# Buffers of the dense matmuls at multiples of 1024 bytes, and another order of the small matmuls in a chunked RWKV-7 solve

## The reference

```
h = rms_norm(x, norm_mix[l])
p = h @ w_in[l]                                   # 2048 -> q, k, v, RWKV inputs, two gates
y_attn = sliding_window_attention(q, k_att, v_att, attn_sinks[l])
y_rwkv = rwkv7_time_mix(r, k, v, dw, da, dg, ...)
merged = (sigmoid(gate_a) * (y_attn @ w_branch_attn[l])
          + sigmoid(gate_b) * (y_rwkv @ w_branch_rwkv[l]))
x = x + merged @ w_out[l]
h = rms_norm(x, norm_ffn[l])
x = x + (silu(h @ ffn_gate[l]) * (h @ ffn_up[l])) @ ffn_down[l]
return rms_norm(x, norm_final)
...
def step(S, inp):                                 # inside rwkv7_time_mix, one token, 16 heads
    sa = einsum('bhij,bhj->bhi', S, -kk_t)
    S = (S * w_t[:, :, None, :] + sa[..., None] * (kk_t * a_t)[:, :, None, :]
         + v_t[..., None] * k_t[:, :, None, :])
    return S, einsum('bhij,bhj->bhi', S, r_t)
```

## Time and profile before

| | us |
|---|---|
| median of 3 runs | 3176.09 |
| their range | 3173.41 to 3176.93 |
| the profiled execution, whole | 3174.01 |
| its span, first to last instruction | 3172.2 |
| TensorE busy in it | 3064.1 (97%) |
| GpSimd / VectorE / ScalarE busy | 1108.0 / 1221.9 / 958.5 |
| TensorE's mean granted clock | 0.987 of 2.4 GHz |

### The profile page before, as it was taken

The page is one execution under the profiler, slowest core; times in us unless marked ns, Lnnn a source line. Parts: engine busy times, 40 slices in busy tenths (PEclk is TensorE's granted clock), DMA queues, the critical chain, the costliest instruction groups (busy, mean ns, idle before and its releaser), DMA issues.

```text
span 3172.2 us, 39005 instructions
## 1 busy us (share of the span) xinstructions
PE 3064.1 (97%) x15226; PEld 2434.3 (77%) x15226; DVE 1221.9 (39%) x1380; ACT 958.5 (30%) x1226; POOL 1108.0 (35%) x275
## 2 busy tenths in 40 slices
PE   7999999999899999999999999999999999999997
PEld 5666777777677777788788888888888888888885
DVE  5446362552535436365554331023211222023345
ACT  4344233332333323322223332133212332122221
POOL 4222122231222212344444444444344443444442
PEclk9999999999999999999999999999999999999998
DMA  4112122121221212334334322222223222222222
GB/s 165 67 67 78 50 77 74 57 83 50 77 72 58 83 48 79 117 139 150 121 139 152 119 94 85 100 105 93 93 91 107 93 93 89 95 106 93 93 86 98
DMA packets 63239, 296.30 MB, mean 93 GB/s; under 512 B 6688, under 2 KB 7968, under 8 KB 38688
## 3 DMA queue, kind: packets, MB, share of 16 engines
q1 hardware_dynamic: 55168, 280.17, 25.1%
q10 hardware_dynamic: 7968, 14.68, 1.2%
HBM read 274.12 MB, written 20.71 MB: 93 GB/s over the span
## 4 chain that ended last, share of the span: by engine, by line
PE 83%; issue 6%; DVE 6%; POOL 2%; ACT 2%; DVEq 1%; DMA 0%; POOLq 0%; SPq 0%; ACTq 0%
PE dense L1173 25%; PE dense L1175 23%; PE dense L1174 23%; PE work L1368 2%; POOL wlo L474 2%; PE work L1349 2%; DVEq L788 1%; DVE zq L970 1%; DVE tmp L838 1%; PE work L1358 1%; DVE tmp L973 1%; PE work L1325 1%; PE work L1228 1%; PE work L1263 1%; PE work L1337 0%
## 5 line engine op out<-in xcount | busy, mean ns | idle before, releaser
L474 POOL TENSOR_TENSOR wlo<-raw,whi 128x2048 fp32r<-128x2048 f32 (+1 forms) x254 | 1083.1, 4264 | 2022.7 <-ACT whi L520 2022.7
L1173 PE MATMUL dense<-H_hi,whi 128*128 128x512 f32 x2672 | 1087.4, 407 | 41.2 <-issue 15.2
L1175 PE MATMUL dense<-H_hi,wlo 128*128 128x512 f32 x2672 | 1049.6, 393 | 0.0
L1174 PE MATMUL dense<-H_lo,whi 128*128 128x512 f32 x2672 | 1048.8, 393 | 0.0
L520 ACT ACTIVATE whi<-raw 128x2048 fp32r<-128x2048 f32 (+1 forms) x255 | 454.2, 1781 | 1482.6 <-PE dense L1175 1404.0
L1173 PEld LDWEIGHTS dense<-H_hi,whi 128*128 128x128 f32 x2672 | 506.0, 189 | 189.0 <-issue 63.4
L1175 PEld LDWEIGHTS dense<-H_hi,wlo 128*128 128x128 f32 x2672 | 506.0, 189 | 109.6
L1174 PEld LDWEIGHTS dense<-H_lo,whi 128*128 128x128 f32 x2672 | 507.3, 190 | 100.9 <-issue 5.0
L1173 PE MATMUL dense<-G_hi,whi 128*128 128x512 f32 x704 | 277.4, 394 | 0.0
L1174 PE MATMUL dense<-G_lo,whi 128*128 128x512 f32 x704 | 277.4, 394 | 0.0
L1175 PE MATMUL dense<-G_hi,wlo 128*128 128x512 f32 x704 | 277.4, 394 | 0.0
(11 more groups left out here) (235 smaller groups left out, 2664.4 us busy)
## 6 DMA issues: line engine op xcount, KB each, us to landing
raw<-w_slots SPq DMA_DIRECT2D x103, 1024.0 KB, 4.9
raw<-w_gu SPq DMA_DIRECT2D x88, 1024.0 KB, 4.7
raw<-w_down SPq DMA_DIRECT2D x64, 704.0 KB, 4.0
gates_dram<-gout ACTq DMA_DIRECT2D x32, 256.0 KB, 2.6
gin<-gates_dram SPq DMA_DIRECT2D x16, 512.0 KB, 3.8
X<-xT SPq DMA_DIRECT2D x8, 512.0 KB, 10.7
xin<-xT SPq DMA_DIRECT2D x16, 256.0 KB, 3.4
x_dram<-x ACTq DMA_DIRECT2D x16, 256.0 KB, 3.6
```

What stands on the lines that cost most here:

```text
L474: nc.gpsimd.tensor_tensor(wlo[s][:, 0:cols], raw[s][:, 0:cols], whi[s][:, 0:cols].bitcast(f32), SUB).then_inc(lo_ready, 1)
L1173: PE.matmul(bank[:], whi[s][:, wk], hi[:, k, :], start=(k == first), stop=False)
L1174: PE.matmul(bank[:], whi[s][:, wk], lo[:, k, :], start=False, stop=False)
L1175: done = PE.matmul(bank[:], wlo[s][:, wk], hi[:, k, :], start=False, stop=(k == last))
```

## The change

It does two things.

1. `cst` and `norm_g` come from an arena of their own (`small`) that begins where `keep` began. `keep` begins behind it, at the next multiple of 1024, 19456 = 19 x 1024. So `raw`, `whi`, `wlo`, `H_hi`, `H_lo` and, since all their sizes are multiples of 1024, `M_hi`, `M_lo`, `G_hi`, `G_lo` and `resid` all begin at multiples of 1024. `cst` keeps its remainder of 128. The other buffers of the pairs move from a remainder of 704 to 896.
2. In the solve, W1 comes first for both heads, the head changing with every product, and the sixteen transposes follow in one block. P2 changes head with every product too. The wait before W1 is now for both heads' masked copies. `w1_done` and `x_done` are raised once per level as before, and `p2_done` twice, both at the end of P2. No instruction of arithmetic is added or taken away.

```diff
+OPERAND_ALIGN = 1024
...
-    keep = Arena(nc, -(-nc.sbuf_base // 64) * 64)
+    small = Arena(nc, -(-nc.sbuf_base // 64) * 64)
+    cst = small("cst", [5, P])
+    ident, ones, head_ones, head_mean, head_center = (cst[:, i, :] for i in range(5))
+    norm_g = small("norm_g", [3, KD])
+    keep = Arena(nc, -(-small.at // OPERAND_ALIGN) * OPERAND_ALIGN)
     raw = [keep(f"raw{s}", [SLOT]) for s in range(2)]
     whi = [keep(f"whi{s}", [SLOT], f32r) for s in range(2)]
     wlo = [keep(f"wlo{s}", [SLOT], f32r) for s in range(2)]
     H_hi = keep("H_hi", [KD, T_SEQ], f32r)
     H_lo = keep("H_lo", [KD, T_SEQ], f32r)
-    cst = keep("cst", [5, P])
-    ident, ones, head_ones, head_mean, head_center = (cst[:, i, :] for i in range(5))
-    norm_g = keep("norm_g", [3, KD])
...
                     for level in range(LEVELS):
-                        for e in range(2):
-                            if level:
-                                pe.wait_ge(p2_read, p * (2 * LEVELS) + 2 * level - 1 + e)
-                            for t in range(NB):
+                        if level:
+                            pe.wait_ge(p2_read, p * (2 * LEVELS) + 2 * level)
+                        for t in range(NB):
+                            for e in range(2):
                                 done = PE.matmul(RW[heads[e], t * HALF:(t + 1) * HALF], Ln[:, e, t, :],
                                                  second_halves(Y[:, e, t, :], level),
                                                  start=True, stop=True)
-                            if e:
-                                done.then_inc(w1_done, 1)
+                        done.then_inc(w1_done, 1)
+                        for e in range(2):
                             for t in range(NB):
                                 at = (e * NB + t) * CHUNK
                                 for c in range(2):
...
-                        for e in range(2):
-                            for t in range(NB):
+                        for t in range(NB):
+                            for e in range(2):
                                 if level < LEVELS - 1 or e + t == 0:
                                     done = PE.matmul(RP[e][:, t * HALF:(t + 1) * HALF],
                                                      Xc[heads[e], t, :], W1[heads[e], t, :],
                                                      start=True, stop=True)
...
-                            done.then_inc(p2_done, 1)
+                                if t == NB - 1:
+                                    done.then_inc(p2_done, 1)
```

## The result

The changed kernel takes 3121.04 us (median of 4 runs, 3117.69 to 3123.4), the kernel before 3175.86 us beside it: a ratio of 0.9828, 95% interval 0.9811 to 0.9845. That is 55 us, not the forecast 175. It lies outside the forecast's own range (2972 to 3025), inside the wide one (to 3130), and on the time of the rival "only the distance between weights and activations matters" (3121 us). The profiled execution took 3117.69 us, with a span of 3115.9; it is the shortest of the four, 3.4 us under their median.

The account below looks back on a forecast made before the run. The prediction took TensorE's own stream of dense matmuls to bound the kernel; alignment 139, W1 and transposes 29, P2 7 summed to 175 us, giving 3001 us, own range 2972 to 3025, 8-in-10 range 2972 to 3130.

Parts of the forecast that it names:

- only the distance between weights and activations matters: Rival for dense matmuls: H stays at 0.2267 us, G and M gain 19 us; 3121 us in all, chance 0.19.
- The reading of the state before: Whole kernel: TensorE, busy 97% of the span, bounds it; 11,280 dense matmuls, read by their distance of starts.
- the excess equals, in cycles, the number of elements between the operand's start and the nearest multiple of 1024 bytes: Dense matmuls: 32 excess cycles for H and 48 for G match their offsets; at remainder 0 the excess is gone.
- 8400 x (226.7 - 215.0) ns = 98 us: Dense matmuls on H: gain claimed from alignment, each falling from 226.7 to 215.0 ns, 98 us.
- 2880 x (233.3 - 215.0) ns = 53 us: Dense matmuls on G and M: gain claimed from alignment, each falling from 233.3 to 215.0 ns, 53 us.
- The deductions for first matmuls, `vbuf` and the rest: Taken off alignment's 156 us: 7 us first matmuls, 6 `vbuf` waits, 3 first tiles and attention, 1 half-clock windows.
- the 5 us for short runs: Dense blocks in the pairs: about 2100 matmuls in short runs gain 2.5 ns more each, 5 us.
- The value 0.215: Assumed us per aligned dense matmul, from f32 matmuls read as two passes; bounds 0.2133 and 0.2267.
- W1 and transposes: Solve: both heads' W1 in 0.61 us, transposes 0.56, level from 1.91 to 1.17; 29 us over 40 levels.
- P2 and the one wait: Solve: P2 from 1.53 to 1.04 us, but W1 waits for both heads' copies; 7 us gained in sum.
- The wait for `vbuf`: In each pair: TensorE's 3.8 us wait at the end of a VectorE chain should grow to 4.5 us.
- collision at every step: Slower rival: weights and activations on multiples of 1024 meet, each dense matmul takes 0.24 us; 3271 us, chance 0.08.

Follow-up runs that it names:

- e14_wlo_128_away: The changed kernel with only the low weights begun 128 bytes (modulo 256) away from the high weights and all activations: 3155.07 us.

## Why the prediction missed

**The reading of the state before** was right: TensorE's stream bounds, and the distance of starts is what to read. Counts and distances stand.

**The step that failed** is "the excess equals, in cycles, the number of elements between the operand's start and the nearest multiple of 1024 bytes". 32 and 48 were a coincidence. What the runs show in its place: the excess hangs on the distance between activations and weights, modulo 256 bytes, and H was at distance 0 before the change already. In the term 8400 x (226.7 - 215.0) ns = 98 us, the 11.7 ns came out as 0; in 2880 x (233.3 - 215.0) ns = 53 us, the 18.3 ns are 6.7. The deductions for first matmuls, `vbuf` and the rest (17 us) went with them, as did the 5 us for short runs. Alignment gave 18 us in place of 139.

| distance modulo 256, bytes | 0 | 4 | 8 | 16 | 32 | 64 | 96 | 128 | 192 | 224 |
|---|---|---|---|---|---|---|---|---|---|---|
| cycles per dense matmul, mean of the three products | 544 | 571 | 560 | 556 | 560 | 549 | 560 | 558 | 560 | 560 |

Weights lay at 0 for the columns 4 to 32, 96 and 224, so these hold for the activations' address as much as for the distance. Before, M and G stood at 192; the change brought them to 0. The output projection to the last product took 1611 us, where 1525 was forecast. The row that should have weighed more was in hand: distances differ in short runs, and the prediction wrote that down for the winning rival but gave it 0.19. Its reason, that the load falls at another moment there, holds only beside the first matmul of such a run (load 107 ns behind its start in the trace of before); at 664.98, where the next start is 0.24 us away, the load starts 3 ns behind as in a steady stretch. Two points can't fix a rule whose modulus and unit are chosen freely; that H stood at the same remainder as the weights, and M and G did not, was the simpler reading.

**The value 0.215** for a matmul without excess was taken from f32 matmuls. No layout here had a mean of the three products under 0.2267. A steady short matmul shows 32 cycles on top of its columns too, so the 0.215 is not what these three-part products reached in any layout tried. The Trainium skill (TensorE: Matmul & The Clock Gate, "Wait — 56ns, not 53.3ns?") has 2.5 ns on top of the columns; by that 512 columns take 215.7 ns, and every such mean over 512 columns here is about 11 ns or more above it.

**W1 and transposes** were right: 0.62 us for the 16 records of W1 (0.61 forecast), 0.57 for the transposes (0.56), the level 1.19 from W1 to dense (1.17). 40 x 0.72 = 29 us, as forecast. That columns' halves run side by side, read from the earlier trace rows, holds for weights of 64 columns as well. The Trainium skill (TensorE: Matmul & The Clock Gate, Part 3, "What overlaps and what doesn't"), by which only another row group lets a load pass, is not borne out: these products use all 128 rows, and so do the dense ones, whose next load starts 3 ns behind the running matmul.

**P2 and the one wait** were right as well. P2 takes 1.04 us (1.04 forecast). From P2 to W1 it is 2.06 (2.08 forecast, 2.42 before) and behind a first level 2.60 (2.58), so there the change costs 0.17. The first copy starts 1.25 us behind P2, not 1.18. The trace shows the wait of 0.60 us only there; the 0.15 us forecast elsewhere is not shown as idle, because the records of the last dense matmuls still drain, though the copy ends at 604.43 and W1 starts at 604.48; from the last dense start to the small block it is 0.46 us before W1 and 0.33 before P2, so some 0.13 us are waited (an estimate from these two). The last level, set at 0, gave 0.10 us per pair in P2 and lost 0.13 to the wait behind it. From the first level's W1 to the last level's a pair takes 20.04 us instead of 23.68, and the last level 0.69 less: 8 x (3.64 + 0.69) = 34.6 us against 36 forecast; the run with the order alone gave 33.5. The 37.2 us between the first and the last W1, with seven last levels in them, hold 3.3 us beside that, of which the shorter time at 1.2 GHz gives about half.

**The wait for `vbuf`** did not grow from 3.8 to 4.5, as its condition, faster dense blocks, did not come. **GpSimd** still idles 6.27 us of a tile, in the kernel after:

```profile
2507.59 4.61 POOL L476 TENSOR_TENSOR wlo<-raw,whi 128x2048 fp32r<-128x2048 f32 x1 [6.27 <-ACT whi L522]
```

**The rival that won** was priced at 19 + 36 us, and measured at 18 and 33.5 alone, 55 together. That the relation of the two operands counts is what happened (that they meet in a bank, as it supposed, was not shown); that the median meets its 3121 to the microsecond is luck, as the four runs spread over 6 us. The rival "collision at every step", forecast at 3271, has it backwards: equal places are the best of those tried, and activations one element off them the worst.

## What to carry over

When a stream of matmuls takes more cycles than columns, look at where both operands begin, since the weights of the next matmul are read while the activations of this one stream; put them at the same place modulo 256 bytes, and measure a shift of one operand alone before believing in an alignment. This was measured for f32r streams with 128x128 weights and 512 columns, not for other shapes or formats. An address rule fitted to two points is a guess: ask first what else the points share. Small products that lie on different halves of the array's rows or columns should change sides each time; then price what waits for all their readers at once.

## What was not expected of the hardware

- The distance between the two operands costs up to 16 cycles per matmul (560 against 544 at 192), repeats every 256 bytes (64 and 320, 128 and 384, 192 and 448 agree within 0.1 cycle), and is not monotonic: activations at 64 cost 5, at 32 and 96 16. Activations 4 bytes past the weights cost 27 (571). At one and the same distance of 64 the three products take 542, 550 and 556 cycles in turn.
- The place of weights that a matmul does not use changes its time: 544 to 558 cycles when only the low weights moved, which are loaded beside it (`e14_wlo_128_away`). The Trainium skill (TensorE: Matmul & The Clock Gate, Part 2, step 1) has it that loads take no bandwidth from the running matmul; this run speaks against that, though by which way the load and the stream meet is open.
- A narrower load is no cheaper: 96 columns in two of three matmuls raised H from 226.7 to 233.6 ns, 64 columns in all raised it to about 229.6.
- At distance 0, 32 cycles per matmul stay, for 512 as for 384 columns. What they are made of is open; no run here took them away.
